# Prompt attention: probabilities turned three steps behind the logits and multiplied five behind, four heads of buffers in both mixers

## The reference

```python
def dense_attention(q, t, k, v, s, tbl, window):
    logits = jnp.einsum('bqgrd,bngd->bqgrn', q, k, ...) * (q.shape[-1] ** -0.5)
    bias = jnp.transpose(tbl[rel_bucket(n)], (0, 2, 3, 1))[None]
    p = masked_softmax(logits + bias, mask[None, :, None, None, :])
    out = jnp.einsum('bqgrn,bngd->bqgrd', p.astype(v.dtype), v)
    return out, p
```

## Time and profile before

| | |
|---|---|
| median of 3 runs | 3421.15 us (3419.18 to 3423.44) |
| the profiled execution, its own time | 3420.26 us |
| its span in the trace | 3418.6 us |
| stage A in the span | 1879.7 to 2082.1 us |
| stage B in the span | 2082.1 to 2206.8 us |

### The profile page before, as it was taken

The page is one execution under the profiler, slowest core; times in us unless marked ns, Lnnn a source line. Parts: engine busy times, 40 slices in busy tenths (PEclk is TensorE's granted clock), DMA queues, the critical chain, the costliest instruction groups (busy, mean ns, idle before and its releaser), DMA issues. The chain is left out here.

```text
span 3418.6 us, 56940 instructions
## 1 busy us (share of the span) xinstructions
PE 3011.9 (88%) x22152; PEld 2644.8 (77%) x22152; DVE 1372.5 (40%) x2236; ACT 709.1 (21%) x1093; POOL 107.2 (3%) x149
## 2 busy tenths in 40 slices
PE   6799999999975889797887676599799999999897
PEld 3599999999963488685454454499699999999897
DVE  2322222212214278465343566643533433334433
ACT  2211111111102021220000343321322222122212
POOL 0000000000000000000000111100000000000000
PEclk8899999999977899998868787799899999999898
DMA  9766676776644631423977233353233333333331
GB/s 339 227 193 172 191 223 196 233 213 207 187 118 133 186 117 50 119 86 125 297 238 229 94 100 105 99 149 95 55 102 95 95 92 98 104 92 113 100 94 50
DMA packets 594868, 496.76 MB, mean 145 GB/s; under 512 B 37148, under 2 KB 515885, under 8 KB 593885
## 3 DMA queue, kind: packets, MB, share of 16 engines
q1 hardware_dynamic: 528408, 408.45, 41.2%
q10 hardware_dynamic: 58496, 60.59, 5.5%
q0 software_dynamic: 7840, 26.10, 1.9%
HBM read 460.02 MB, written 48.70 MB: 149 GB/s over the span
## 5 line engine op out<-in xcount | busy, mean ns | idle before, releaser
L146 PE MATMUL psum<-h_high,w_high 128*128 128x260 f32 x4992 | 1014.1, 284 | 21.7 <-DVE w_low L133 21.7
L146 PE MATMUL psum<-h_high,w_low 128*128 128x260 f32 x4992 | 1007.9, 284 | 0.0
L146 PE MATMUL psum<-h_low,w_high 128*128 128x260 f32 x4992 | 1006.1, 283 | 0.0
L146 PEld LDWEIGHTS psum<-h_high,w_high 128*128 128x128 f32 x4992 | 770.6, 189 | 62.8 <-ACT pj_out L558 29.3
L146 PEld LDWEIGHTS psum<-h_high,w_low 128*128 128x128 f32 x4992 | 771.3, 189 | 0.0
L146 PEld LDWEIGHTS psum<-h_low,w_high 128*128 128x128 f32 x4992 | 769.5, 189 | 0.0
L133 DVE TENSOR_TENSOR w_low<-w,w_high 128x2048 fp32r<-128x2048 f32 x162 | 370.9, 2291 | 561.6 <-ACT w_high L128 561.6
L128 ACT ACTIVATE w_high<-w 128x2048 fp32r<-128x2048 f32 x162 | 309.1, 1909 | 466.6 <-PE psum L146 361.9
L600 DVE COPY pj_out<-psum 128x260 f32<-128x260 f32 x66 | 28.3, 429 | 485.1 <-PE psum L146 485.1
L558 ACT ACTIVATE pj_out<-psum 128x260 f32<-128x260 f32 x66 | 25.6, 387 | 636.6 <-PE psum L146 636.6
L199 PE MATMUL psum<-w,c 128*32 128x512 f32 x768 | 110.9, 659 | 25.9 <-DMA w<-in_w_ada 17.8
(11 more groups left out here) (369 smaller groups left out, 2826.8 us busy)
## 6 DMA issues: line engine op xcount, KB each, us to landing
w<-in_w_ada SPq DMA_DIRECT2D x96, 1024.0 KB, 6.4
w<-in_w_in_att SPq DMA_DIRECT2D x65, 1024.0 KB, 9.3
w<-in_w_in_conv SPq DMA_DIRECT2D x64, 1024.0 KB, 6.3
proj<-pj_out POOLq DMA_DIRECT2D x66, 260.0 KB, 5.3
cz_pgk<-in_cache_nsa_cmp_k SPq DMA_DIRECT2D x128, 128.0 KB, 2.1
cz_pgv<-in_cache_nsa_cmp_v SPq DMA_DIRECT2D x128, 128.0 KB, 2.2
w<-in_w_out_att SPq DMA_DIRECT2D x16, 1024.0 KB, 6.6
w<-in_w_out_conv SPq DMA_DIRECT2D x16, 1024.0 KB, 6.3
```

Source lines behind the costliest of these rows:

```text
L146: mm = pe.matmul(k.psum[:, banks + hf, 0:HC], w[:, kt, :], x[:, kt, hf * HC:(hf + 1) * HC], start=(kt == 0 and m == 0), stop=(kt == KT - 1 ...
```

## The change

```diff
-    SL = 2 if A else 4
+    SL = 4
...
-    DP, DT, DV, ring = 1, 2, 3, 4
+
+    DP, DT, DV, ring = 1, 3, 5, 4
...
-        hvc = k.sb("pa_vc" + tag, [NCB // 4, 2, P], ctx=ctx)
+        hvc = k.sb("pa_vc" + tag, [NCB // 4, SL, P], ctx=ctx)
...
-                        v = t - (2 if A else 1)
+                        v = t - 2
                         if 0 <= v < U and v % UH < ZP:
                             recip_z(g, units[v][0], v % UH)
```

## The result

The changed kernel takes 3395.41 us (median of 4 runs, 3391.63 to 3397.38) where the kernel before takes 3421.08 (4 runs). The ratio is 0.9926 with a 95% interval of 0.9911 to 0.994: 25.7 us faster, where 33 had been forecast. The profiled execution has a span of 3395.7 us.

The account below looks back on a forecast made before the run. It took stage A's load waits, with the low clock behind them, as the loss and VectorE as the next bound; 28 us from stage A plus 5 from stage B gave 3388 us, range 3379 to 3403.

Parts of the forecast that it names:

- What bounds it: Prompt attention's stages A and B, 327 us: gains pass to the end; load waits and TensorE's low clock slow stage A.
- Heads 1 and 2: Middle heads of a stage A group: 23.8 and 24.9 us become 17.2 each, a gain of 14.3 per group.
- waits that stay: Stage A's middle heads: 0.5 us taken off the gain for each of two heads, 1.0 per group.
- Head 0: First head of a stage A group: 19.2 us becomes 18.2, gain 1.0, bounds 0 and 2.0.
- The end of a group: Stage A, behind the last turning: one more product of six matmuls lies open, loss 0.9 us per group.
- What the distances give: More steps between logits, turning and product loosen the loop through TensorE and VectorE; in stage B alone, gain 4.6 us.
- The rival of the loads: Only the loads matter: stage A gains 17.4 us, stage B nothing, 3404 us; chance 0.20.
- The upper bound of stage A, 34: Stage A's largest gain, 34 us: VectorE the bound from the first unit on, no waits that stay.
- Stage B: Second stage of prompt attention: shorter `qk` waits and moved VectorE and GpSimd collisions, gain 5 us, bounds 11 and loss 2.
- The rival of the clock, slower: Stage A's heads: small gaps at VectorE's pace hold TensorE's clock at 0.50, 46 us later, 3466; chance 0.03.

Follow-up runs that it names:

- the finish-first kernel: The changed kernel with `finish` ahead of the z reciprocals in VectorE's step; one run, stage A 170.3 us for 175.3.
- the kernel with the old distances: Changed kernel's four slots, but distances 1, 2, 3 as before the change: 3397.88 us; with the three edits as well, 3395.82 us.
- the three edits: Changed kernel with `finish` ahead of the z reciprocals, GpSimd's store one head later, stage B's z reciprocals one step earlier: 3377.30 us, ratio 0.9865.
- the filling: Two unread products in TensorE's standstill at stage A's group ends; on the changed kernel stage A 172.0 us, with the three edits 3377.12 us.
- four slots alone: The changed kernel with only stage A's four slots, distances and place of z reciprocals as before: 3397.88 us, ratio 0.9926.

## Why the prediction was right, and where it was off

- **What bounds it: right.** The stages pass what they gain to the end, 26.6 us by their lengths and 25.7 by the medians. The four waits for loads went, and the clock in heads 1 and 2 of the first group is 1.00 and 0.99 for 0.88 and 0.77. (The prediction also gives this clock in GHz; the rows show a share only, and the argument needs no more.)
- **Heads 1 and 2: right.** Forecast 17.2 us and 0.5 for waits that stay, measured 17.6 to 18.0. What stayed is not a wait, though: 0.77 us of it is the second instruction of `finish` beside GpSimd's product, 0.92 us for 0.16, as the finish-first kernel shows with heads of 17.1 to 17.3.
- **Head 0: too small.** 1.0 us forecast, 3.3 and 1.4 measured. It is in part work put off: TensorE executes 56 matmuls in it where the kernel with the old distances executes 65, and does the rest later. Most of it is saved all the same once the end is cheap: with the three edits and the filling, both heads 0 together are 6.3 us shorter than with the old distances and both ends 2.1 longer.
- **The end of a group: the step that failed.** I had "a loss of 0.9, one more product". It lost 3.7 and 2.1 us in stage A, 3.4 and 3.1 in stage B. In stage A the product itself (it is that of unit 29, as long as the one named) is 0.6: 22 matmuls take 2.62 us at a clock of 1.00, 16 took 2.01. Most of the rest is the clock, which the forecast had left at 1.00 there: TensorE runs ahead of VectorE, stands still for 2.92 us and does the backlog partly at 0.50, 6.96 and 5.21 us from the turning of unit 30 on in place of 4.19. Filling the standstill gave back 1.0 us at each end, no more than the ends of one program differ by. With the edits of order it gave back 1.6 and 0.8, with the clock at 1.00 to the last product of both ends. The ends are then 9.6 and 11.8 us against 8.6 and 10.7 with the old distances, so 1.0 and 1.1 longer: with the standstill gone, the forecast's 0.9 is about right. In stage B the last multiplication is stretched by 1.1 us (1.58 for 0.49), where 0.5 had been taken; what else is in its end was not taken apart.
- **What the distances give: wrong.** The forecast gave them 10 us of stage A (28 less the loads' 17.4) and nearly all of stage B. The loads alone bring the whole gain, since the clock's part belongs to them too; the distances save 0.7 us of waiting per head (1.3 to 2.0 in some) and gave it back in collisions and at the ends. The rival of the loads had this right, and was wrong by its 17.4: four slots alone bring 27 us. So the total fell near the forecast in part by luck: the loads' part was taken 9 us too small, and that of the distances 15 us too large. The upper bound of stage A, 34, also leaves out the 0.9 at each end; with it, it is 32.
- **Stage B: 1.7 us for 5.** Right: the 2.12 us multiplications went, the wait for `1 + e` came (0.77 us in four heads, and 0.24 in the multiplication before it, 1.0 as forecast). Off: the maximum of 128 keys is stretched by 0.88 (1.17 for 0.29) and not 0.75, and the ends as above.
- **The rival of the clock, slower:** in heads 1 and 2 the clock is 1.00 and 0.99, in the second group 1.00 and 0.98, with TensorE's small gaps there. It was 0.50 behind the standstill at the first group's end (1966.5 to 1973.2), and for 3.0 us in the last head of each group (1949.5 to 1952.5 and 2031.5 to 2034.5), where no idle time just ahead was longer than 0.91 us; so it did not fall behind a halt alone. A loss by the clock was there, but for the most part not where this rival had it.

## What to carry to other kernels

Find out first which waits are for loads, and give them buffers before deepening a pipeline: the distance between stages is paid for at each end of it, and a later finish frees buffers later. After moving a step, look for the instructions of two engines that now fall together; here three exchanges of order, with no instruction less, took 13.9 us from the changed kernel's stages (3.3 with the old distances), and only with them did the depth pay. A gain in the first unit of a pipeline is to be checked against its last, because it may be in part the same work done later. And how far one program's stage differs between executions is to be known before two stages are compared.

## What the hardware showed that I had not expected

- A VectorE instruction over 8 columns took 0.92 us in place of 0.16 and ended 0.02 us after the GpSimd product beside it (1962.73 to 1963.65, the product 1962.35 to 1963.63); with `finish` first, ahead of the product, it took 0.16. The length of the instruction alone said nothing about this cost.
- GpSimd's `1 + e` can be the longer one: it took 1.95 us for 1.51 where it began beside a masked maximum of 512 keys (2099.67 in the trace of before), and the multiplication after that maximum kept its length, 0.42 us for 384 keys (2100.55; the mean of the eight in stage B is 0.42).
- TensorE's clock was 1.00 and 0.99 through heads in which TensorE was busy for 14.9 of 17.5 and 15.3 of 17.9 us, and 0.50 in the first 12.6 us of a group, busy for 10.6. The share of busy time is much the same, 0.85, 0.86 and 0.84; ahead of the last the engine had stood still for 13.6 us, up to 1891.5, at the barrier and the first loads.
